# Side products of a recurrence's gates in pieces of 32 and 64 result columns

## The reference, cut to what matters

```python
D_RNN = 5 * D_MODEL // 4          # 2560
N_GATE_BLOCKS = 16
GATE_BLOCK = D_RNN // N_GATE_BLOCKS   # 160

def rglru_block(u, w_in, conv_w, conv_b, w_r, b_r, w_i, b_i, lam, w_out):
    B, L, _ = u.shape
    proj = u @ w_in
    gate = jax.nn.gelu(proj[..., :D_RNN])
    xr = causal_depthwise_conv(proj[..., D_RNN:], conv_w, conv_b)
    xb = xr.reshape(B, L, N_GATE_BLOCKS, GATE_BLOCK)
    r = jax.nn.sigmoid(jnp.einsum('blnc,ncd->blnd', xb, w_r).reshape(B, L, D_RNN) + b_r)
    i = jax.nn.sigmoid(jnp.einsum('blnc,ncd->blnd', xb, w_i).reshape(B, L, D_RNN) + b_i)
    log_a = -LRU_C * r * jax.nn.softplus(-lam)
    a = jnp.exp(log_a)
    bvals = jnp.sqrt(-jnp.expm1(2.0 * log_a)) * (i * xr)
    _, hs = lax.associative_scan(_linear_combine, (a, bvals), axis=1)
    return (hs * gate) @ w_out
```

## Time and profile before

| what | us |
|---|---|
| device time, median of 3 runs | 3256.52 |
| lowest and highest of them | 3251.93, 3256.79 |
| the profiled execution | 3252.73 |
| its span, first to last instruction | 3250.9 |

### The profile page before, as it was taken

How to read it: one execution, slowest core, us unless ns; L and a number is a source line. 1 busy time by engine, 2 the same in 40 slices (tenths; PEclk the granted TensorE clock), 3 DMA queues, 4 the chain that set the end, 5 groups by cost and what they waited for, 6 DMA issues and landing times.

```text
span 3250.9 us, 59566 instructions
## 1 busy us (share of the span) xinstructions
PE 3198.9 (98%) x25789; PEld 3101.3 (95%) x25789; DVE 1891.5 (58%) x1696; ACT 1509.4 (46%) x1596; POOL 183.9 (6%) x164
## 2 busy tenths in 40 slices
PE   8999999999999999999999999999999999999998
PEld 8998889999789999999999999999988999999998
DVE  7755554767777655554544445555776555545454
ACT  5455553656556754443433334433454434434343
POOL 1140000000021200000000000100001000000001
PEclk9999999999999999999999999999999999999999
DMA  7564443899764455555655555555434666666664
GB/s 252 157 189 136 143 133 123 279 291 302 269 223 150 137 169 173 177 175 176 179 181 173 177 181 179 179 169 180 149 124 143 194 194 194 194 192 193 192 194 147
DMA packets 552496, 598.39 MB, mean 184 GB/s; under 512 B 9920, under 2 KB 531136, under 8 KB 552320
## 3 DMA queue, kind: packets, MB, share of 16 engines
q1 hardware_dynamic: 550416, 589.18, 57.6%
q0 software_dynamic: 1760, 6.59, 0.7%
q10 hardware_dynamic: 144, 0.01, 0.0%
HBM read 593.64 MB, written 2.10 MB: 183 GB/s over the span
## 4 chain that ended last, share of the span: by engine, by line
PE 87%; DVE 6%; ACT 3%; DMA 2%; issue 1%; SPq 0%; POOL 0%; DVEq 0%; ACTq 0%; POOLq 0%
PE acc L621 24%; PE acc L626 23%; PE acc L624 23%; DVE low L1926 2%; PE psx L1186 1%; PE acc L1088 1%; PE acc L1090 1%; PE acc L1089 1%; ACT high L1342 1%; DMA raw<-in_w_expert_gate 1%; PE acc L1171 1%; PE psx L1171 1%; PE acc L1169 1%; PE psx L1169 1%; PE psx L1170 1%
## 5 line engine op out<-in xcount | busy, mean ns | idle before, releaser
L621 PE MATMUL acc<-gh,high 128*128 128x256 f32 (+1 forms) x4416 | 899.5, 285 | 5.6 <-DVE low L1926 3.9
L624 PE MATMUL acc<-gl,high 128*128 128x256 f32 (+1 forms) x4416 | 885.8, 282 | 0.0
L626 PE MATMUL acc<-gh,low 128*128 128x256 f32 (+1 forms) x4416 | 885.8, 282 | 0.0
L2213 DVE TENSOR_TENSOR low<-raw,high 128x2048 fp32r<-128x2048 f32 x264 | 605.1, 2292 | 399.7 <-ACT high L1578 399.7
L1926 DVE TENSOR_TENSOR low<-raw,high 128x2048 fp32r<-128x2048 f32 x261 | 606.2, 2326 | 331.9 <-ACT high L1342 331.4
L1578 ACT ACTIVATE high<-raw 128x2048 fp32r<-128x2048 f32 x264 | 505.4, 1914 | 494.4 <-DMA raw<-in_mlp_w 486.8
L621 PEld LDWEIGHTS acc<-gh,high 128*128 128x128 f32 x4416 | 680.6, 188 | 17.4 <-issue 8.4
L626 PEld LDWEIGHTS acc<-gh,low 128*128 128x128 f32 x4416 | 678.5, 189 | 0.0
L624 PEld LDWEIGHTS acc<-gl,high 128*128 128x128 f32 x4416 | 676.4, 188 | 0.0
L1342 ACT ACTIVATE high<-raw 128x2048 fp32r<-128x2048 f32 x261 | 498.6, 1913 | 315.6 <-DMA raw<-in_w_kv 67.9
L621 PE MATMUL acc<-fh,high 128*128 128x272 f32 (+1 forms) x2048 | 408.9, 281 | 0.0
(11 more groups left out here) (471 smaller groups left out, 3587.3 us busy)
## 6 DMA issues: line engine op xcount, KB each, us to landing
raw<-in_mlp_w SPq DMA_DIRECT2D x256, 1024.0 KB, 5.4
raw<-in_w_in SPq DMA_DIRECT2D x59, 1024.0 KB, 5.3
raw<-in_a_w_in SPq DMA_DIRECT2D x40, 1024.0 KB, 5.0
raw<-in_w_expert_up SPq DMA_DIRECT2D x32, 1024.0 KB, 5.9
raw<-in_w_expert_down SPq DMA_DIRECT2D x32, 1024.0 KB, 5.2
raw<-in_w_kv SPq DMA_DIRECT2D x32, 1024.0 KB, 5.5
raw<-in_w_expert_gate SPq DMA_DIRECT2D x28, 1024.0 KB, 5.7
raw<-in_a_w_out SPq DMA_DIRECT2D x20, 1024.0 KB, 5.0
```

Source lines behind the costliest of these rows:

```text
L621: pe.matmul(o[n], hw[:, k, c[n]], h, start=first and not (packed and n), stop=False, skip_group_check=packed)
L624: pe.matmul(o[n], hw[:, k, c[n]], l, start=False, stop=False, skip_group_check=packed)
L626: m = pe.matmul(o[n], lw[:, k, c[n]], h, start=False, stop=last, skip_group_check=packed)
L2213: dve.tensor_tensor(tile(low, k, k % SLOTS), tile(raw, k, k % SLOTS), tile(high, k, k % SLOTS).bitcast(F32), ALU.subtract)\
```

## The change

For each result tile `b`, a list `SIDES[b]` names the pieces of the side products: the 128 result columns are cut where the neighbouring gate block changes, in pieces of 32, 64 or 128 columns.

| b | pieces as (input tile, first column, columns) |
|---|---|
| 0 | (1, 0, 128) |
| 1 | (0, 0, 32), (2, 32, 32), (2, 64, 64) |
| 2 | (1, 0, 64), (3, 64, 64) |
| 3 | (2, 0, 64), (2, 64, 32), (4, 96, 32) |
| 4 | (3, 0, 128) |

The block computes the full product of tile `b` with itself first, and adds each piece to its own partitions of the bank, which are its column group of the array. Parts of the two side products that are zero throughout are no longer multiplied. The waits, the semaphores and the bank are the same; the diff also draws the tile with itself ahead of its lower neighbour.

```diff
+def side_pieces(b):
+
+    of = [[a for a in range(SUP) if a != b and P * a < RBLK * (m + 1) and P * a + P > RBLK * m]
+          for m in ((P * b + 32 * g) // RBLK for g in range(4))]
+    out, g = [], 0
+    while g < 4:
+        n = next(n for n in (4, 2, 1) if g % n == 0 and all(of[g + x] == of[g] for x in range(n)))
+        out.append((of[g][0], 32 * g, 32 * n))
+        g += n
+    return out
+
+
+SIDES = [side_pieces(b) for b in range(SUP)]
...
-                meets = [a for a in range(SUP) if BC[a] <= P * b < BC[a] + BWID[a]]
                 for j in range(2):
-                    for a in meets:
-                        c = BOFF[a] + P * b - BC[a]
-                        m = pe.matmul(psx[:, 2 * j + t % 2, 0:TB], band[:, j, c:c + P], xr[:, SUP * g + a, :],
-                                      start=a == meets[0], stop=a == meets[-1])
+                    for a, at_, n in [(b, 0, P)] + SIDES[b]:
+                        c = BOFF[a] + P * b - BC[a] + at_
+                        m = pe.matmul(psx[at_:at_ + n, 2 * j + t % 2, 0:TB], band[:, j, c:c + n], xr[:, SUP * g + a, :],
+                                      start=a == b, stop=a != b)
                 m.then_inc(rg_mm, 1)
```

## The result

The changed kernel takes 3260.24 us in the median of 20 runs, the kernel before 3254.88 us in the median of its 20; the ratio is 1.0018, with a 95% interval from 1.0012 to 1.0024. By the ratio that is 5.9 us (3.9 to 7.8), by the medians 5.4 us. It is slower by a hair less than the 0.2% at which the prediction drew its line.

The account below looks back on a forecast made before the run. PE, busy for 98% of the span, was taken to bound the kernel. -0.95 us (b=2) and +7.5 us (b=1, b=3) gave +6.6 us on 3256.52, so 3263.1 us, with a range of 3252 to 3267.

Parts of the forecast that it names:

- The sum: Gate blocks: -0.95 us at b=2 plus +7.5 us at b=1 and b=3, together +6.6 us.
- The inner switch: Between 32- and 64-column pieces at b=1 and b=3: a 0.13 us stop and second round, +0.47 us a case.
- the way into a narrow width: PE going from full to narrow products: it empties before the first narrow weight load, costing 0.13 us.
- The counter-example: Outside the gates, 15-column transposes led into full weights without a stop: a narrow column count alone forces none.
- Rival 1: At b=1 and b=3 the widths overlap, all 24 cases cost 0.80 us: -2.9 us, 3253.6 us; chance 0.13.
- rivals 2 and 3: Gate pieces run in turn, +17.3 us, chance 0.05; or all overlap without any stop, -11.0 us, chance 0.02.
- The base: The +6.6 us was added to the median of three timed runs before, 3256.52 us, not to the profiled 3252.73.
- The waits for the band: PE's three waits for the band's DMA between groups were to stay at 2.4 us, their chain being untouched.
- What is late next: Gate blocks of b=1 and b=3 end 0.94 us later; ScalarE, GpSimd and VectorE follow, keeping their distance to PE.
- a frame: Around a narrow block on PE: about 0.33 us, 0.13 on the way in and 0.20 on the way out.

Follow-up runs that it names:

- the sorted order: The change's own pieces, both gates' full products first, then all 32-column pieces, then all 64-column ones; ratio 1.0002 against the kernel before.
- the one width: The changed kernel with the 64-column pieces of b=1 and b=3 cut into two of 32; ratio 0.9997 against the kernel before.
- b=2 alone: The changed kernel with full side products again at b=1 and b=3, only b=2 narrow; ratio 1.0002 against the kernel before.
- the frame alone: The kernel before with the full side product of b=0 and b=4 cut into two 64-column pieces; ratio 1.0020 against the kernel before.
- the faster form: As the one width, plus both gates' full products first, then their narrow pieces, in one frame; ratios 0.9989 and 0.9987 in two runs against before.

## Why the prediction was right

**The sum.** +6.6 us was forecast, and the blocks grew by 6.6 us. Its terms hold one by one, and no two errors cancel in it: b=2 was put at -0.12 us a gate and read -0.11; b=1 and b=3 at +0.47 and read +0.47. The blocks were forecast at 1.85, 2.51 and 3.69 us and came to 1.85, 2.53 and 3.68.

**The inner switch** was the step without a row. The value taken, 0.13 us as on the way into a narrow width, was right: the stop is 0.09 us here too, and the sorted order and the one width both showed that it is paid and that it forbids the overlap. The counter-example named in the prediction, the 15-column transposes that led into full weights without a stop, did not apply to these products: whether transposes keep the full width whatever their columns, no run tested. Rival 1, with its 3253.6 us, fell in the profile of the change itself; rivals 2 and 3 fell with the block of b=2, at 2.53 us and not at 3.4 or 1.85.

**The base.** 3263.1 us against 3260.24: the forecast stood on the median of three runs, 3256.52, and the median of 20 is 3254.88. That is 1.6 of the 2.9 us. The other 1.2 us lies between +6.6 and the medians' +5.4, inside the interval. The forecast stood on the line of 0.2%, so the sum could not tell on which side of it the result would fall.

**The waits for the band** were said to stay at 2.4 us, because the change touches neither end of their chain. That step was too firm: they read 2.0 us after the change and in the sorted run, 3.1 with b=2 alone, 3.0 with one width, 3.2 and 3.7 with one frame, 1.4 with the frame alone. In the last, 0.6 us has a reason, since three blocks of b=4 now end in a way out of 0.20 us that covers part of the transfer. The rest goes with single DMA issues and landings: with b=2 alone, for one, the last DMA ahead of the third group took 3.48 us to land, against 2.50 before. The forecast came out 0.4 us too high by it, and the faster form had 0.8 to 1.3 us more of these waits.

**What is late next.** ACT waited longer for the gates, 11.9 instead of 8.7 us, and PE did not wait for ACT: its own list in the stage still has the band alone. That holds for the change; in the faster form, whose blocks are shorter, PE met a wait for ACT of 0.3 us.

## What to carry to other kernels

In this kernel narrow products on separate column groups pay by the round, and each change of width around them costs about 0.13 us on the way in and 0.20 us on the way out: count the changes of width in program order, not the pieces. Give all pieces of a place one width, even if that means more pieces, and gather the pieces of several results behind one change. Two products of 272 float32 columns replaced by one round barely pay for a frame (0.11 us of 0.92 are left); where one is replaced by one, the frame is a loss.

## What was not expected of the hardware

That the price is so even: 0.09 us from the end of the stream to the next load for 128 to 32, 32 to 64 and 64 to 128 columns alike, and that the blocks with narrow pieces, where nothing held them up, repeat to 0.01 us. And one and the same small DMA of the band took SP 0.59 us to issue in most groups and 1.81 us in one of the faster form's, with nothing in the trace to account for it.
